# SSD projection and z_b as one loop of 128-column blocks in three rounded parts

## The reference

```python
proj = h @ W["w_in_even"][e]
q_a, g_a, kv_a, z_a, z_b, xbc, dt_raw = _split(proj, EVEN_SPLIT)   # z_b 1024 columns, xbc 1536, dt 16
...
for i in range(SSD_CONV):                                          # 4 taps along the tokens
    conv = conv + xp[:, i:i + s] * cw[i]
xs, bm, cm = _split(jax.nn.silu(conv), [1024, 256, 256])
dt = jax.nn.softplus(dt_raw + bias)
y, new_ssd = ssd_scan(xs, dt, a, bm, cm, h0)                       # chunk after chunk: the state h goes along
y = y + xs * d
y = y * jax.nn.silu(z_b)
y = rms_norm(y, W["ssd_norm_w"][e])
out = concatenate([o_a, y]) @ W["w_out_even"][e]
```

## Time and profile before

| | us |
|---|---|
| three timed runs, median | 2158.56 (2151.85 to 2159.27) |
| the profiled execution, its own time | 2153.33 |
| its span | 2151.6 |
| TensorE busy | 1876.8, 87% of the span |
| VectorE, ScalarE, GpSimd busy | 693.7, 524.9, 286.9 |
| mean granted clock of TensorE | 0.935 |

### The profile page before, as it was taken

How to read it: one execution, slowest core, us unless ns; L and a number is a source line. 1 busy time by engine, 2 the same in 40 slices (tenths; PEclk the granted TensorE clock), 3 DMA queues, 4 the chain that set the end, 5 groups by cost and what they waited for, 6 DMA issues and landing times. The chain is left out here.

```text
span 2151.6 us, 25397 instructions
## 1 busy us (share of the span) xinstructions
PE 1876.8 (87%) x10730; PEld 1266.2 (59%) x10730; DVE 693.7 (32%) x1200; ACT 524.9 (24%) x1001; POOL 286.9 (13%) x209
## 2 busy tenths in 40 slices
PE   4499949699889799979997959997999999978795
PEld 4245537366666566656665547774668855534694
DVE  1321110256555234434443231114301124432524
ACT  1400110155444321123343200015311112320004
POOL 1011000011100000024453420000000000010410
PEclk9699979889999899999998979998999999988898
DMA  9101083100000101200001454333110010004312
GB/s 345 72 0 68 1 204 84 42 1 2 1 1 1 44 20 40 98 4 1 1 1 30 124 175 149 110 121 143 40 39 20 20 40 1 1 30 137 120 40 81
DMA packets 116901, 131.83 MB, mean 61 GB/s; under 512 B 15926, under 2 KB 93912, under 8 KB 116148
## 3 DMA queue, kind: packets, MB, share of 16 engines
q1 hardware_dynamic: 95572, 104.94, 15.3%
q10 hardware_dynamic: 20864, 25.17, 3.4%
q0 software_dynamic: 352, 0.10, 0.1%
HBM read 104.83 MB, written 27.43 MB: 61 GB/s over the span
## 5 line engine op out<-in xcount | busy, mean ns | idle before, releaser
L154 PE MATMUL banks<-h_T,w_xbc 128*128 128x352 f32 x576 | 170.9, 460 | 0.0
L154 PE MATMUL banks<-w_attn,h_T 128*128 128x512 f32 (+5 forms) x432 | 160.1, 533 | 0.0
L154 PEld LDWEIGHTS banks<-h_T,w_xbc 128*128 128x128 f32 x576 | 109.5, 190 | 60.9 <-issue 0.6
L154 PE MATMUL banks<-w_r,h_T 128*128 128x512 f32 (+1 forms) x288 | 129.0, 602 | 0.0
L154 PE MATMUL banks<-w_z_b,h_T 128*128 128x512 f32 (+1 forms) x288 | 126.2, 597 | 0.0
L154 PE MATMUL banks<-w_qkv,h_T 128*128 128x256 f32 (+1 forms) x576 | 125.6, 380 | 0.5 <-ACT h_T L2045 0.5
L154 PEld LDWEIGHTS banks<-w_attn,h_T 128*128 128x128 f32 (+1 forms) x432 | 78.5, 183 | 80.3 <-issue 63.5
L154 PEld LDWEIGHTS banks<-w_qkv,h_T 128*128 128x128 f32 (+1 forms) x576 | 103.9, 181 | 22.4 <-issue 2.6
L154 PE MATMUL banks<-h_T,w_qkv 128*128 128x352 f32 x384 | 114.5, 460 | 0.0
L1143 DVE TENSOR_REDUCE neg_max_att<-banks 128x1 f32<-128x640 f32 (+7 forms) x128 | 89.2, 702 | 73.7 <-PE banks L154 73.4
L154 PE MATMUL banks<-conv_T,out_even_w 128*128 128x352 f32 x288 | 92.0, 470 | 14.2 <-DMA out_even_w<-in_w_out_even_dram 12.9
(11 more groups left out here) (427 smaller groups left out, 2977.4 us busy)
## 6 DMA issues: line engine op xcount, KB each, us to landing
out_even_w_mod<-in_w_mod_dram ACTq DMA_DIRECT2D x8, 2048.0 KB, 9.5
h_T<-x_T_save SPq DMA_DIRECT2D x2, 4224.0 KB, 16.8
w_qkv<-in_w_in_odd_dram SPq DMA_DIRECT2D x8, 1024.0 KB, 5.4
w_xbc<-in_w_in_even_dram SPq DMA_DIRECT2D x6, 1024.0 KB, 5.3
x_T_save<-x_T SPq DMA_DIRECT2D x1, 4224.0 KB, 23.6
x_T_save<-h_T SPq DMA_DIRECT2D x1, 4224.0 KB, 19.2
xin<-in_x_prompt_dram SPq DMA_DIRECT2D x2, 2048.0 KB, 16.0
h_T<-in_w_mod_dram SPq DMA_DIRECT2D x2, 2048.0 KB
```

Source lines behind the costliest of these rows:

```text
L154: return nc.tensor.matmul(out, lhsT, rhs, start=start, stop=stop, skip_group_check=True)
```

## The change

- The projection loop runs over 20 blocks of 128 columns (`SSD_COLS`): the 12 of xBC, then the 8 of z_b. All are computed in three rounded parts. ScalarE rounds a block of weights (`high_w`), GpSimd takes the rest (`rest_w`), and TensorE waits for it once a block.
- h is split once: ScalarE writes `h_T_high`, VectorE writes the rest over `h_T` itself, third by third, after the dt matmuls have read it.
- silu(z_b) is written feature-major to `silu_z_T` by ScalarE straight from the banks. In the scan and in the samples block, TensorE turns it to rows by eight transposes, which ScalarE copies (a copy, no silu).
- The weights of the first two blocks are loaded during the attention block ahead; the others in pieces of 512 KB, each when the block two before it is done. The small loads for dt go first.
- The last columns are turned and stored under the first z_b blocks instead of at the end.
- The mask `bmask` is no longer kept: both samples blocks load it at their start.

```diff
@@ block_ssd_proj
 @block.sync
+sp.dma_start(wdt...); sp.dma_start(fold_in...)
 sp.dma_start(prow[:, :], e.state_ssd_conv[0].rearrange("b t c -> (b t) c")).then_inc(prev_in, 16)
-for c in range(KC // 2):
-    if c >= 2:
-        sp.wait_ge(proj_done, 6 * (c - 1))
-    ...
-sp.dma_start(S.w_zb[:, :, :], ...).then_inc(S.w_zb_in, 16)
+for f in range(2, NF):
+    sp.wait_ge(proj_done, 3 * (f - 1))
+    load_w_ssd(sp, e, S, f)
 @block.tensor
+def group(f, c):
+    g, (s, n) = 3 * f + c, CHUNKS[c]
+    if g >= 6:
+        pe.wait_ge(taken, g - 5)
+    if f == 0:
+        pe.wait_ge(h_high, 2 * (c + 1))
+        pe.wait_ge(h_rest, 2 * (c + 1))
+    if c == 0:
+        pe.wait_ge(w_rest, f + 1)
+    out = e.ps[:, g % 6, 0:n]
+    for k in range(KD):
+        mm(nc, out, whi[:, f % 2, k, :], hhi[:, k, s:s + n], k == 0, False)
+        mm(nc, out, whi[:, f % 2, k, :], hlo[:, k, s:s + n], False, False)
+        last = mm(nc, out, wlo[:, f % 2, k, :], hhi[:, k, s:s + n], False, k == KD - 1)
+    last.then_inc(proj_done, 1)
...
+for f in range(1, NF):
+    for c in range(3):
+        group(f, c)
+    if f == KC:
+        last_rows(0)
+        last_rows(1)
+    if f == KC + 1:
+        last_rows(2)
 @block.scalar
-for f in range(KC):
-    if f >= 2:
+for f in range(NF):
+    if f + 1 < NF:
+        high_w(f + 1)
+    if 2 <= f < KC:
         act.wait_ge(conv_done, f - 1)
         act.wait_ge(kept, f - 1)
     for c, (s, n) in enumerate(CHUNKS):
         g = 3 * f + c
         act.wait_ge(proj_done, g + 1)
+        if f >= KC:
+            nc.scalar.activation(S.zT[:, f - KC, s:s + n], e.ps[:, g % 6, 0:n], ACT.Silu).then_inc(taken, 1)
...
+    if KC < f <= KC + 3:
+        b = f - KC - 1
+        act.wait_ge(cv_turned, b + 1)
+        nc.scalar.copy(cvrow[:, b * 512:(b + 1) * 512], e.ps[0:27, 6 + b % 2, :]).then_inc(cv_copied, 1)
@@ block_ssd_scan, TensorE's unit z and ScalarE's taking of it
-for c in range(2):
-    for k in range(KD):
-        last = mm(nc, e.ps[:, b + c, :], hT[:, k, tok], w[:, k, 512 * c:512 * (c + 1)], k == 0, k == KD - 1)
+for j in range(8):
+    last = nc.tensor.transpose(e.ps[:, b + j // 4, (j % 4) * P:(j % 4 + 1) * P], S.zT[:, j, tok], e.ident)
-nc.scalar.activation(zs[:, i % 2, :].rearrange("p (b n) -> p b n", b=2), both("z", i), ACT.Silu).then_inc(taken["z", "act"], 1)
+nc.scalar.copy(zs[:, i % 2, :].rearrange("p (b n) -> p b n", b=2), both("z", i)).then_inc(taken["z", "act"], 1)
```

More of the change, by code:

```diff
@@ L990, in block_attn_prompt, with _ @@
         with nc.Block() as block:
+            @block.sync
+            def _(sp):
+                for f in range(2):
+                    load_w_ssd(sp, e, S, f)
             @block.tensor
@@ L1207, in block_ssd_proj @@
[L1207 to L1210, removed]
@@ L1265, in _ @@
-                pe.wait_ge(kept, KC)
-                pe.wait_ge(raw_ready, NG)
-                for f in range(KC):
-                    last = nc.tensor.transpose(e.ps[0:27, f // 4, (f % 4) * P:(f % 4 + 1) * P], cv[:, f, :], e.ident)
-                last.then_inc(cv_turned, 1)
+                group(0, 0)
+                pe.wait_ge(part_ready, 3)
+                for m in range(NT):
+                    last = mm(nc, e.ps[0:rows(m), 7, m * SH:(m + 1) * SH], dtp[:, m * P:m * P + rows(m)], fold_in[:, :], True, True)
@@ new lines, in _ @@
+                last.then_inc(dt_done, 1)
+                group(0, 1)
+                pe.wait_ge(prev_in, 16)
+                for f in range(KC):
+                    last = nc.tensor.transpose(e.ps[:, 6, f * 24:(f + 1) * 24], prow[:, f * P:(f + 1) * P], e.ident[0:24, 0:24])
+                last.then_inc(prev_done, 1)
+                group(0, 2)
+                for f in range(1, NF):
[6 more added lines that the diff above has]
+                        last_rows(2)
@@ L1650, in _ @@
                 last.then_inc(xs_done, 1)
-                for c in range(2):
-                    for k in range(KD):
-                        last = mm(nc, e.ps[0:R, 2 + c, :], hT[:, k, tok], S.w_zb[:, k, 512 * c:512 * (c + 1)], k == 0, k == KD - 1)
+                for j in range(8):
+                    last = nc.tensor.transpose(e.ps[0:R, 2 + j // 4, (j % 4) * P:(j % 4 + 1) * P], S.zT[:, j, tok], e.ident)
                 last.then_inc(z_done, 1)
@@ L1920, in layer_even @@
             early.close()
-            block_attn_prompt(nc, e, A)
-        S = Env()
+            S = Env()
+            S.w = early.enter_context(nc.sbuf_tensor("w_ssd", [P, 2, KD, P], F32, side="right"))
+            S.w_in = [nc.alloc_semaphore(f"w_ssd_in{i}") for i in range(2)]
+            block_attn_prompt(nc, e, A, S)
+        early.close()
+        S.w_rest = early.enter_context(nc.sbuf_tensor("w_ssd_rest", [P, 2, KD, P], F32R, side="right"))
         with ExitStack() as ctx:
```

161 lines of the change are left out of this document (91 added, 70 removed).

## The result

The changed kernel takes 2176.41 us (median of 5 runs, 2170.01 to 2179.89), the kernel before, run beside it, 2156.54 (5 runs): a ratio of 1.0088, 95% interval 1.0065 to 1.0112. It is slower by 20 us; the forecast was 2182 from a typical 2156. The profiled execution took 2172.73 us, its span 2170.9 us, with a mean granted clock of 0.916 (before: 2153.33, 2151.6 and 0.935), so the two profiled executions differ by 19.4 us, nearly what the medians differ by.

A forecast was written before the change was run, and what follows sets the result against it. TensorE's stream bounds projection and scan; without z_b's cover, the normalisation chain and low clock set the chunk. 49.7 - 18.8 - 3.6 = +27.3 on a typical 2156 gave 2182 us, range 2149 to 2194.

The forecast's parts named there:

- The projection, +49.7: Projection block: twenty blocks of 11.45 us on TensorE move the scan's start from 933.4 to 983.1, +49.7 us.
- the 4.4 us that the weights leave: Projection: loading and preparing a block's weights takes 7.0 us of 11.45, so it is hidden with 4.4 us to spare.
- The chunk, 26.6 us: Scan: one chunk takes 20.5 us of chain plus 6.1 us for the low clock, 26.6 us.
- The chain of 20.5 us: Scan chunk: TensorE from turning y to cum1, then VectorE and ScalarE normalising y, at least 20.5 us at full clock.
- The clock's 6.1 us: Scan chunk: after 5.3 us of TensorE idle, 12.3 us of work run at half speed, costing about 6.1 us.
- The scan, -18.8: Scan: 15.1 us start, seven chunks 186.2 and 22.6 end make 223.9 us against 242.7, -18.8 us.
- The samples' block, -3.6: Samples block: states start 5.9 us earlier without z matmuls, about 2.3 us lost to a cold start, -3.6 us.
- (A): Scan: the clock comes back soon, 22.6 us a chunk, kernel 2155 us; chance 0.22.
- (B): Scan: the clock does not fall in the 5.3 us of idle, kernel 2138 us; chance 0.10.
- (C): Scan: the clock never comes back between idle stretches, 33.0 us a chunk, kernel 2228 us; chance 0.04.
- (D): Projection: slower than the odd layer's through late weights or copies, kernel 2190 to 2200 us; chance 0.04.
- The Trainium skill's oscillation rule: Scan: bursts parted by idle stretches each start at half clock, so the change trades matmul work for cold starts.

The follow-up runs named there:

- run 10: Changed kernel with the projection's third part (the weights' rest times the high part of h) left out: 2123.31 us, ratio 0.9827.
- run 1: Changed kernel plus six unread 512-column matmuls a chunk ahead of TensorE's wait to turn y, in seven chunks: 2142.38 us, ratio 0.9929.
- run 3: Kernel before, with only the scan's z_b matmuls replaced by eight transposes of x's columns, projection and samples unchanged: 2136.00 us, ratio 0.9897.
- run 7: First: changed kernel plus four unread matmuls in the samples, 2176.83 us. Second: run 6 plus seven there and one ahead of intra, 2117.31 us.
- run 9: First: run 8 with ScalarE's copy of x ahead of the exponential, 2127.59 us. Second: that plus seven unread matmuls in the samples, 2119.14 us.
- run 2: Changed kernel plus 48 unread transposes a chunk in the place where run 1 has six matmuls: 2146.46 us, ratio 0.9941.
- run 4: Changed kernel with the turning of y moved behind the intra matmuls and state update, no work added: 2126.62 us, ratio 0.9855.
- run 6: Run 4 plus one unread 512-column matmul between the two halves of the intra matmuls: 2115.97 us, ratio 0.9808.
- run 8: Run 4 with the state update moved ahead of the intra matmuls, no work added: 2120.38 us, ratio 0.9826.

## Why the prediction was right, and what was off

**The projection, +49.7: measured +49.4.** The dt matmuls start at 738.95 (739.5), and from there it is 243.9 us to the scan (243.6). The block time taken from the odd layer's projection was 11.45 for a measured 11.53; the 1.6 us that this makes over 20 blocks were made up by smaller terms (the wait ahead of the last four turned columns was 1.0 us for 1.4, the small transposes and the fold a little less than put down), so the closeness of the sum is in part luck. The spare time of a block was not the 4.4 us that the weights leave, though: in run 10 the ring of convolution and silu closes a block at 9.74 us. If it takes as long beside three parts, only 1.8 us were left in the blocks of xBC. It cost nothing, but it was not in the working.

**The chunk, 26.6 us: measured 26.1.** Its two halves were tested apart. The chain of 20.5 us is the 20.42 of run 1. The clock's 6.1 us are 5.7: low stretches of 10 to 14 us against the 12.3 taken, ahead of them 4.6 to 5.5 us of idle against 5.3.

**The scan, -18.8: measured -26.9.** The 8 us have three parts. From the first intra matmuls to the last it is 181.2 us instead of 186.2, 5.0 less. Ahead of the first it is 9.5 us instead of 15.1, 5.6 less: I let them wait for both halves of the decay matrix and kept the times of a scan that starts behind 10 us of idle. TensorE comes at full clock from the projection now, and its intra starts with the first half, at 992.27, the second following 2.75 us later. Run 3, which keeps the idle end of the projection, needs 2.9 us more up to there. From the last intra matmuls to the end it is 25.2 us instead of 22.6, 2.6 more.

**The samples' block, -3.6: measured -0.8.** The mechanism was right and the term mis-sized. The states do start 6 us sooner after the block's start (18.0 against 24.0 us), and TensorE waits for GpSimd's operand there. But I gave the low clock 2.3 us, and it lasted from 1196.8 to 1227.6, over the turnings and two states: those cost 14.8 us instead of 9.7, which alone is 5.1. The kernels with seven matmuls in that gap (the second ones of runs 7 and 9) put those two states back to full speed.

**The sum.** It was +27.3, and the parts come to 49.4 - 26.9 - 0.8 = +21.7, or +19.3 with the unchanged rest. The scan's 8 us and the samples' 3 err in opposite directions. A small slip is in the last step too: +27.3 on a typical 2156 is 2183, not 2182.

**The rivals.** (A), the clock back soon, would have had low stretches of 4.3 us and a chunk of 22.6; they were 10 to 14 us. (B), the clock does not fall, is what run 1 made by filling the gap, at 2142 for a forecast of 2138. (C), clock never back, did not come: it was at 1.00 for 13.7 us in each chunk, and run 2 shows that transposes hold the clock. (D) did not come. The Trainium skill's oscillation rule (TensorE: Matmul & The Clock Gate, HAM oscillation), with which the prediction went, was borne out by run 1. The length of the idle time is not all, though: run 4 lost the clock with 1.08 us of idle in a chunk, and runs 6 and 8 kept it with 1.25 and 2.4. The prediction had the short matmuls in mind only for how long the clock stays low, not for whether it falls.

**What decided.** z_b was moved from a place where it covered a chain of other engines to one where nothing needs cover. Uncovered, the chain set the chunk, and the gap in TensorE's line brought the half clock. TensorE's busy time in both blocks together did not change: 181.7 + 228.8 us before, 241.3 + 168.8 after. The projection took on 59.6 us; the scan lost 8 times 12.86, or 103 us of work, and the low clock gave 43 of them back. In a chunk it was busy 21.8 us at the mixed clock (windows 1067.1 to 1093.9); in run 1 the same work is 20.4 less the six added matmuls of 0.86, or 15.2.

## What to carry to other kernels

Work on the busiest engine that covers a chain of other engines is worth, when it is taken away, only the difference to that chain, and here the idle stretch cost a further 5.7 us a chunk through the clock: price the chain first, then the clock behind the gap. Once the cover is gone, the order inside the loop becomes worth something: the same reordering gave 0 us before the change and 50 after it, and with one filling matmul the changed kernel reached 0.981 of the kernel before. A gap of TensorE that can't be closed may be filled with other work: matmuls and transposes both held the clock here; but look at the whole program, since in run 7 6 us won in one block did not show in the time.

## What the runs showed of the hardware

- TensorE's granted clock fell in each chunk of run 4, with a gap of 0.26 us (once 0.89) ahead of eight heads of short matmuls (64 columns) and one of 0.78 us between them and the next eight. It stayed at 1.00 when 0.94 us of long matmuls stood between the two halves (most chunks of run 6, with 1.23 us of idle ahead of them), when the same short matmuls followed other work without a gap (runs 1 and 2), and in most chunks of run 8, with 1.90 and 0.50 us of idle elsewhere in the chunk. So the sum of idle time does not tell whether the clock falls; what about the gap between short matmuls does it was not isolated.
- VectorE and GpSimd hold each other up. A copy of 128x16 took 0.17 us alone and 2.05 beside a GpSimd product, ending with it; an operation from PSUM (L1600) took 1.22 us in either case. The Trainium skill (SBUF — State Buffer, SBUF: two separate sides) calls it an exclusive lock on a shared pair of ports that lasts for a whole instruction; the trace agrees, with the 2.05 us and with VectorE's 17.3 instead of 14.1 us a chunk in run 9.
- The unchanged 900 us behind the samples' block took from 898.4 to 909.0 us in different executions, with the same instructions; in the two windows of run 7 TensorE's busy time and mean clock differ and the other engines' busy times agree within 0.2 us. It is enough to hide a gain of 6 us.
